# Layer two's queries in two groups of two tiles, with a second pass over the query weights

## What is computed

```python
q = (xb @ wq).reshape(tb, 8, 2, 128)                # wq: 1024 x 2048
s1, s2 = q[:, :, 0] @ k1.T, q[:, :, 1] @ k2.T       # 128 keys each
v1, i1 = top_k(s1, 16); v2, i2 = top_k(s2, 16)
top_s, pos = top_k(v1[..., :, None] + v2[..., None, :], 16)
eid = take(i1 * 128 + i2, pos)                      # 8 heads x 16 experts a token
w = gelu(xb . expert_u[eid]) * softmax(top_s)
out = sum_k w[k] * expert_v[eid[k]]
```

## Time and profile before

| what | us |
|---|---|
| median of three runs | 4717.45 (4716.44 to 4719.75) |
| the profiled execution | 4714.7 |
| its span, first to last instruction | 4712.8 |
| PE busy in the span | 3117.5 (66%) |
| DVE busy | 3124.9 (66%) |
| ACT busy | 901.5 (19%) |
| POOL busy | 1497.8 (32%) |

### The profile page before, as it was taken

One profiled execution on the slowest core, in us unless ns is written; L12 is line 12 of the kernel. 1 busy time (PEld: TensorE's weight loads), 2 busy tenths in 40 slices (PEclk: granted clock), 3 DMA queues, 4 the chain that ended last, 5 costly groups with the idle time before them and its releaser, 6 DMA issues.

```text
span 4712.8 us, 48940 instructions
## 1 busy us (share of the span) xinstructions
PE 3117.5 (66%) x16288; PEld 1204.9 (26%) x16288; DVE 3124.9 (66%) x8345; ACT 901.5 (19%) x2458; POOL 1497.8 (32%) x1376
## 2 busy tenths in 40 slices
PE   6889988756885555554554678787895555555554
PEld 2445454311321111111111223545431111111111
DVE  1251336778777778778778862524587877877886
ACT  1341311111111111111112111521111111111211
POOL 0000012334434444444443430001244444444443
PEclk8999979877997787777776888997998777776777
DMA  4242315999999999999999991012699999999998
GB/s 148 92 165 76 132 49 211 414 411 405 417 418 399 420 413 405 417 416 405 418 415 381 403 418 45 12 54 90 254 415 394 411 420 413 402 418 413 400 417 351
DMA packets 295132, 1502.98 MB, mean 319 GB/s; under 512 B 25600, under 2 KB 85376, under 8 KB 131040
## 3 DMA queue, kind: packets, MB, share of 16 engines
q0 software_dynamic: 185888, 1347.13, 69.5%
q1 hardware_dynamic: 77504, 121.14, 7.6%
q10 hardware_dynamic: 31488, 31.60, 2.0%
HBM read 1487.11 MB, written 12.66 MB: 318 GB/s over the span
## 4 chain that ended last, share of the span: by engine, by line
DVE 41%; PE 27%; DMA 19%; issue 7%; ACT 4%; POOL 1%; DVEq 1%; SPq 0%; ACTq 0%; POOLq 0%
DMA X<-in_uv_dram,X 18%; DVE X L1852 17%; PE ps L514 8%; PE ps L1008 6%; DVE X L1863 2%; ACT X L1412 2%; DVE X L1751 1%; DVE X L1753 1%; DVE X L1754 1%; DVE X L1859 1%; PE ps L945 1%; PE ps L797 1%; PE ps L787 1%; POOL X L1984 1%; PE ps L758 1%
## 5 line engine op out<-in xcount | busy, mean ns | idle before, releaser
L1008 PE MATMUL ps<-X 64*64 64x512 f32 x2560 | 1643.2, 775 | 1331.8 <-DVE X L1863 1328.1
L1984 POOL DMA_INDIRECT X<-in_uv_dram,X x1280 | 1421.8, 1111 | 2138.5 <-PE ps L1011 1661.5
L1852 DVE CUSTOM_DVE_ANT_0 X<-yT,X 128x1024 f32<-128x1024 f32 x1280 | 1532.3, 1223 | 327.3 <-DMA X<-in_uv_dram,X 294.6
L1011 PE MATMUL ps<-X 64*64 64x512 f32 x2560 | 1643.5, 776 | 0.0
L1010 PE MATMUL ps<-X 64*64 64x512 f32 x2560 | 1643.4, 776 | 0.0
L1009 PE MATMUL ps<-X 64*64 64x512 f32 x2560 | 1643.4, 776 | 0.0
L1008 PEld LDWEIGHTS ps<-X 64*64 64x64 f32 x2560 | 359.7, 163 | 2539.4 <-DVE X L1863 1879.7
L1412 ACT ACTIVATE X<-X 128x1 f32<-128x1 f32 x1280 | 258.1, 203 | 2334.0 <-DVE X L1852 2308.1
L1011 PEld LDWEIGHTS ps<-X 64*64 64x64 f32 x2560 | 359.9, 163 | 0.0
L1010 PEld LDWEIGHTS ps<-X 64*64 64x64 f32 x2560 | 359.9, 163 | 0.0
L1009 PEld LDWEIGHTS ps<-X 64*64 64x64 f32 x2560 | 359.7, 163 | 0.0
(11 more groups left out here) (276 smaller groups left out, 3427.3 us busy)
## 6 DMA issues: line engine op xcount, KB each, us to landing
wring<-in_ada_w_dram SPq DMA_DIRECT2D x48, 1024.0 KB, 5.4
wring<-in_w_in_dram SPq DMA_DIRECT2D x28, 1024.0 KB, 5.5
wring<-in_peer_wq_dram SPq DMA_DIRECT2D x24, 1024.0 KB, 25.6
X<-in_uv_dram,X POOLq DMA_INDIRECT x1280
wring<-in_w_out_dram SPq DMA_DIRECT2D x8, 1024.0 KB, 5.1
X<-scores ACTq DMA_DIRECT2D x64, 128.0 KB
X<-mods ACTq DMA_DIRECT2D x15, 512.0 KB, 9.0
scores<-X ACTq DMA_DIRECT2D x16, 256.0 KB, 15.0
```

Of the source, the lines that this page charges most:

```text
L1008: pe.matmul(ps[0:HD, h, :], dg(slice(0, HD), s), v0[0:HD], **ends)
L1011: m = pe.matmul(ps[0:HD, 2 + h, :], dg(slice(HD, P), s + 1), v1[HD:P], **ends)
L1852: v.tensor_tensor_reduce(uvr[:, slot, 0:D], h2[:, t, :], uvr[:, slot, 0:D], 1.0, 0.0, ALU.mult, ALU.add, adot[:, s_:s_ + 1]).then_inc(S("d ...
L1984: g.indirect_dma_start(uvr[:, slot, :], None, a["uv"], bass.IndirectOffsetOnAxis(ap=istages[i % 2][:, s:s + 1], axis=0)).then_inc(S(f"uv{s ...
```

## The change

Layer two's tiles are split 2 and 2 where they were 4 and 0. Through `groups(L)` this reaches all engines: the first group's queries cover two tiles, expert tile 1 makes the rest group's 128 query blocks, SP sends the eight halves of `wq` once more behind the first eight, the stores are of one tile in expert tile 0 and of two in expert tile 1, and `rows_early` is three where it was four. The fourth row is then normed in the midst of the head's choices, so GpSimd waits for it ahead of slot 2. The wait of layer one keeps its count and place.

```diff
-FIRST_GROUP = (CT, TILES - CT)
+FIRST_GROUP = (CT, CT)
@@ gathers(i), GpSimd @@
-                        if L < LAST and i == 0 and s == 5:
-                            g.wait_ge(S("n_h"), nb_(1, L) + TILES)
+                        if i == 0 and s == (2 if L else 5):
+                            g.wait_ge(S("n_h"), nb_(1, L) + TILES - lo)
                             g.sem_inc(S("asked"), 1)
```

## The result

The changed kernel is slower by about a quarter of a per cent: 4730.13 us median (4725.57 to 4735.89, 13 runs) against 4721.01 of the kernel before in the same series (4712.99 to 4724.04, 13 runs), a ratio of 1.0024 with a 95% interval of 1.0016 to 1.0032. At 4721 us that is 11.3 us (7.6 to 15.1); the two medians by themselves are 9.1 us apart. Forecast were 9.1 us, and a time of 4726.6 in a range of 4718.5 to 4735.5. The profiled execution took 4731.62 us. It lies 16.9 us over that of before, but 4.2 us of these were there before anything that the change touches: the last residual add (L1712, into the stream `xs`) ahead of the expert part begins at 3326.27 instead of 3322.05. So from here on I measure from that add.

The account below looks back on a forecast made before the run. The prediction took plain expert tiles to be bound by the bytes the DMA moves, near 412 GB/s. Head -1.4, tile 0 -7.3 and tile 1 +17.8 made +9.1 us on 4717.45: 4726.6, range 4718.5 to 4735.5.

Parts of the forecast that it names:

- the head: Layer two's start: fourth row's norm leaves the path to head 0's choice, so the first gather comes 1.44 us earlier.
- tile 1: Layer two's expert tile 1: 7.34 MB more for second pass and stores, paid by bytes, +17.8 us (17.8 to 18.4).
- tile 0: Layer two's expert tile 0, first gather to fold: 365.0 us instead of 372.34, 7.3 less, as lost DMA time returns.
- case A: The sum of head, tile 0 and tile 1: +9.1 us, 4726.6, range 4722 to 4731; chance 0.60.
- case C: Second pass and stores pay for packets, not bytes: tile 1 costs 22.1 us, sum +13.4, 4730.9; chance 0.14.
- lost DMA time: Layer two's tile 0, check by bytes: 20.4 us second pass, less 9.8 lost there, less 1.4, plus 0.6: +9.8.
- the later steps hold more work on PE: Layer two's tile 0: second reason given for its lost DMA time, PE busy 266.02 against 230.57 us.
- The wait for the store: Layer two's tile 0: VectorE's 16.38 us wait stays but is covered; release 11 us earlier, at 3379.
- the packets' price: By queue rows: weights 2.92 us a MB, stores 3.22; layer one's tile 1 would be 38 us longer, is 30.77.
- TensorE's addition: Layer two's tile 1: 256 matmuls of 415 ns, some 70 us on top of 174.84, hidden under the DMA.
- B: Layer two's tile 0 gives nothing back, the gain's broadcast still holding the stores: +16.4 us, 4733.9; chance 0.12.
- D: Layer two's tile 0 gains by its earlier first dot product, ending 14.6 us earlier: sum +3.2, 4720.7; chance 0.14.

Follow-up runs that it names:

- both broadcasts moved: Changed kernel with the gate row's broadcast issued at step 8 of layer two's tile 0 and the final gain's in tile 1; ratio 1.0022 to the kernel before.
- tiny stores: Changed kernel with the rest group's 16 stores in layer two cut to 16 of 128 partitions; 4734.34 us, single run.
- both cuts: Changed kernel with an eighth of the second pass's bytes and the rest group's stores cut to 16 of 128 partitions; 4714.22 us, single run.

## Why the prediction was right, point by point

**The number.** The measured 4730.13 us lie in the range and near the 4726.6 forecast, and 3.6 us of the distance are the kernel before itself, whose median was 4717.45 of three runs and 4721.01 of thirteen. That the two medians differ by just the 9.1 us of the sum is in part luck: the two profiles differ by 12.7 from the add on, and the errors lie in the head (+0.4 against -1.4), in tile 1 (+19.2 against +17.8) and in tile 0 (-6.4 against -7.3), all on one side. The time alone doesn't speak for case A either, since case C had 4730.9; the stages have to decide.

**What bounds the kernel.** Right. Cutting the second pass's bytes, with all its matmuls and copies left in, takes the time back to that of the kernel before.

**The head.** The mechanism is right and the size near: 1.24 us where TensorE ran at full clock, 1.44 in the sum. The profiled run didn't have it. The step that was missing is the clock: I took layer one's 12.59 us from the score matmuls on and forgot that the way to the score matmuls can vary too.

**Expert tile 0.** -6.4 us against -7.3, and by the mechanism named first, VectorE's wait for the stores: moving the gain alone gives 5.9 of it, shorter stores alone 4.7. Of the first some 1.3 us are bytes moved to another tile, of the second some 2 us are bytes left out ahead of step 12. Two sentences were wrong. Of the 9.8 us of "lost DMA time" in the check by bytes, what came back lies ahead of step 12. The diagonal matrices of that step, in the kernel before and in the changed one:

```profile
3432.44 0.29 DVE L1863 TENSOR_TENSOR X<-wukv,X 128x128 f32<-128x128 f32 x1
```

```profile
3430.00 0.29 DVE L1863 TENSOR_TENSOR X<-wukv,X 128x128 f32<-128x128 f32 x1
```

They are 89.5 and 82.4 us behind the first gather, 7.1 us apart, and from there to the fold it is 282.9 and 283.5 us; over all twelve profiles this second part takes 281.0 to 285.1 us, and the lowest two are those with 2.75 MB less in the tile. And "the later steps hold more work on PE" explained nothing: with that work kept, tile 0 was 4.7 us shorter.

The wait for the store went as forecast: VectorE was released 38.2 us behind the first gather (forecast 37.5) and lost nothing by it, which the run with both broadcasts moved shows.

**Expert tile 1.** +19.2 us against +17.8, and against the plain tile behind it 19.6, 17.7 and 17.6 in the three profiles with the whole second pass and the broadcasts in place. So the term was right or up to 2 us too small; the profiles can't say which. What it was made of was not right. The weights cost 2.5 to 3.2 us a MB and not 2.42, and their own queue has 2.86 in this tile, close to the 2.92 of case C; the stores that were cut cost 1 to 2.8 us, less than the 4.5 of their bytes. The two errors offset each other, which is luck. So case C was near on the weights and wrong on the stores, and I had dismissed both by one sum. Layer one's tile 1 may stay under the packets' price for the same reason, its 4.19 MB of stores hardly counting; layer one itself wasn't changed in any run. TensorE's addition was sized too large, at 70 us: it was busy for 226.51 us against 174.84, 51.7 more. That changed nothing, since it was hidden.

By the Trainium skill, DMA: Bandwidth & Descriptors, section "Why small descriptors are slow (HBM only)", a packet has a fixed overhead of about three cycles, and from that the prediction had estimated 8% for runs of 1 KB. The direction is confirmed by the run with 8 KB runs. The size is more: q1's price in this tile was 2.86 us a MB in 1 KB runs and 2.37 in 8 KB runs, 21% apart, and tile 1 was 1.9 to 2.4 us shorter, 13 to 16% of the 15.0 us that q1 took there.

**The rivals.** B, tile 0 gives nothing back: wrong, with the wait covered as argued. C: its time, 4730.9, is the nearest of all to what was measured, but it had tile 1 at 350.9 us, and that was 347.4 to 348.0; half right, as above. D, tile 0 gains by its first dot product: wrong; the dot product came 13.6 us behind the first gather, as worked out, and the tile was not 14.6 but 6.4 us shorter. Up to step 12 the changed kernel moves 409 GB/s, so there its bytes bind and not its start.

## What to carry to other kernels

Where a stage runs at the DMA's full rate, a second pass over weights costs its transfer, however many matmuls are hidden under it; the price by the queue's own rows (here 2.86 us a MB) came nearer than the price by bytes (2.42), and stores priced in the same way came out too dear. In a stage with dips the same transfer can be cheap: here 2.75 MB cost 2.1 us. A dip in the DMA's rate is worth something only if the stage's end moves when it goes: ask whether the time from there to the end would change. And look at what stands in the same queue ahead of a small transfer that someone waits for: here a broadcast that wasn't needed in that tile held it, and moving that one line gave nearly as much in tile 0 as the whole change, without the second pass. Last, measure a stage against a like stage of the same profile before you believe a difference of a microsecond or two.

## What the runs showed of the hardware that I had not expected

TensorE's clock in the short stretch of the first queries differs from profile to profile. First the changed kernel, then the run with most of the second pass left out, in the stretch of the same matmuls (there 2 us earlier):

```profile
3329.00:3335.00 6.00, 5.48 (x34) 5.50 (x34) 3.45 (x5) 0.66 (x3) 0.00 (x0) 0.72 0.18 65
```

```profile
3327.50:3331.30 3.80, 3.78 (x34) 3.80 (x34) 2.96 (x5) 0.28 (x1) 0.00 (x0) 1.00 0.16 56
```

The columns are those of the earlier trace rows; the third from the end is the granted clock, 0.72 against 1.00, so part of the stretch ran at the lower level, 1.2 GHz instead of 2.4: from 3330.5 to 3333.5 it was 0.50. The 32 matmuls there take 5.44 us or 3.81. In both TensorE had stood idle for 3.15 us just before. All five kernels with four rows first had the fast form. Of the seven profiles with three rows first, the four whose second pass is the changed kernel's own had the slow one (the changed kernel twice, with both broadcasts moved, and with tiny stores), and the three with another second pass had the fast one. In both its profiles the changed kernel thus loses 1.6 us here, and its head is 0.4 us later than before instead of 1.2 earlier.

It would be wrong to put this down to the second pass or to the three rows. These first queries come before the second pass does anything. And the same 32 matmuls at layer one's head, which the change doesn't touch, also take 5.44 us in the changed kernel's own profile, and 3.81 in the kernel before:

```profile
761.89 5.44 PE L906 MATMUL ps<-hT,wring 128*128 128x128 f32 x32 [3.14 <-ACT hT L1325]
```

Layer one's are slow in six profiles: those four, and the ones with 8 KB runs and with both cuts, whose layer two was fast. In these six the stretch begins at 761.1 to 763.0 us and in the other six at 755.5 to 757.6; most of the lag is there within the first 63 us of the program: VectorE's last addition at L1494 there starts at 61.1 to 62.9 us in the six and at 56.8 to 58.2 in the others. So the slow clock at layer one's head goes with something that is settled early in an execution, and layer two's was slow only where layer one's was. Whether that comes with a build of the kernel or by chance, and why the clock falls, stays open: each kernel but the changed one has one profile.
